# Two attentions of a second transformer block on one Trainium2 core: outputs with features on partitions, value products in pairs, and the forgetting attention alone before the output projection

## Chip, cores and metric

The kernel runs on one core of one Trainium2 chip. It is one launch that computes two transformer-like blocks on 512 tokens of width 1024, in float32. The metric is the device time of the launch in microseconds, the median of three runs. The sizes that recur below: 128 partitions, 64 features per head, query blocks of 128 tokens.

## What is computed

The first block (window attention, a long convolution by Fourier transform, differential attention, gates and a feed-forward part) is untouched by the change. The second block is this:

```python
h = rmsnorm(x, attn_norm_g)
fq, fk, fv, f_logit, sq, sk, sv = split(h @ w_in)      # 8 heads of 64 in each kind
# forgetting attention ("fox"), causal, softmax over keys
logits = fq . fk / 8 + F[t] - F[s];   p = softmax(logits, s <= t);   o_fox = p @ fv
# stick-breaking attention ("stick"), strictly causal, a reversed running sum over keys
z = sq . sk / 8
A = exp(log_sigmoid(z) + sum over s < j < t of log_sigmoid(-z[t, j]));   o_sb = A @ sv
o = concat(rmsnorm(o_fox) * fox_out_g, rmsnorm(o_sb) * sb_out_g)       # each over 512 features
x = x + o @ w_out
x = x + (silu(gate) * val) @ w_down      # gate, val = conv3(rmsnorm(x) @ w_up)
return rmsnorm(x, final_norm_g)
```

## The kernel before

**Dense products.** Every product with a weight matrix is a "group" of slots. A slot is two 128-row tiles of the weight, 512 columns wide. SyncE streams it from memory into `wraw`, ScalarE rounds it to a high part `whi` (L1489), VectorE subtracts to get the low part `wlo` (L863), and TensorE multiplies three times (high with high, low with high, high with low), so that a slot costs 24 products with 512 columns. The activations are kept the same way: `hThi`/`hTlo` for the normed input, `ohi`/`olo` for the attentions' output, `achi`/`aclo` in the feed-forward part.

**Work beside it.** The class `Flow` interleaves that with step-wise work. `Flow.pump(n)` advances the first generator of the list `beside` by n steps in each slot; `rate` of a group is that n, and the steps are spread over a slot's blocks. `Flow.drain()` runs what is left with no products between. All five engine programs (`tensor_program` for PE, `vector_program` for DVE, `scalar_program` for ACT, `gpsimd_program` for POOL, `sync_program` for SP) run the same groups and generators in the same order, so a step has one place on every engine. Nothing else sets the order.

**The two attentions.** `stick()` has 37 steps and `fox()` 38; each handles 32 units, a unit being one head of one query block n (its keys are 128 (n + 1) wide). A unit of `stick()` runs through: scores (PE, into bank 4 or 5, with a masking product), copy `zb` (ACT L1791), `parts` (DVE L1299, L1300), two logarithm steps (ACT L1796, L1798), running sum `sums` (DVE L1307), addition (POOL L2158), exponential (ACT L1803), `turn` (PE: up to four 128x128 transposes of `Lb` into bank 6), `evac` (DVE L1315, to `PT`) and `values` (PE, `PT` as the stationary side, 64 columns of `sv` moving). A unit of `fox()`: scores (PE `Kf,Qf`), row minimum `lowest` (DVE L1340), exponential with its sum (ACT L1832), `turn`, evacuation (DVE L1348 for even units, ACT L1840 for odd ones) and `values` with `fv`. Its score banks in the drain are 0, 1 and 2, its turns go to banks 4 and 5 by turns, and its values to 6 and 7. It stops at step 3 until `fox_go`, which is set after the group fv.

Both attentions run a query block at a time through their norms. Values lie with tokens on partitions, so for each block ACT squares and sums, POOL makes the root and scales (L2143), PE turns four tiles back (`out_norm_turn`), and ACT (L1781) and DVE (L1269) write `ohi` and `olo`. The fox softmax is divided once per block, in that path (L1356, L1361).

**The order around it.** Groups of the second block: sq, sk, fl (the forgetting logits, with a small running sum), sv at rate 1, fq at rate 2, fk at rate 4, fv at rate 4, each of 4 slots save fl; then the drain of `fox()`; then the output projection, `xs0`/`xs1` for the stick half of its rows and `xf0`/`xf1` for the fox half, into one set of banks; then the token norm (POOL's squares `sqs`, L2103 and L2105, PE's `token_squares` and `spread_roots`), 11 groups vp and two groups vd, in which `x_back` adds the residual by products of `xT` with the identity.

```python
def pump(self, n=1):
    for _ in range(n):
        if self.beside:
            try:
                next(self.beside[0])
s_units = [(n, h) for n in (3, 0, 2, 1) for h in range(8)]
pairs = [(n, h) for two in ((3, 0), (2, 1)) for h in range(8) for n in two]
group("fq", hT, h_ready(2), ..., 2)
group("fk", hT, h_ready(2), ..., 4)
```

Of the kernel before, what the change touches and what calls it, by code (L numbers as in the profile page):

```python
# [136 lines left out]
def counts(run):  # L137

    done, bank, n, turn = {}, {}, 0, 0
    for name, nk, cols, mode in run:  # L140
        done[name] = n
        n += 4 if mode == "tok" else cols // 128
        two = name[:2] in ("wo", "up", "dn", "xs", "xf", "vp", "vd")
# [8 lines left out]
def build(nc, d, out):  # L152
# [26 lines left out]
    def col(name, i=0, n=1, p=128):  # L179
# [89 lines left out]
    PT2 = [sb(f"PT2_{i}", AR + 124 + 2 * i, [128, 512]) for i in range(2)]  # L269
# [16 lines left out]
    in_vec, in_z, in_w3, in_dec, in_tab, in_inv = (  # L286
        sem(n) for n in ("in_vec", "in_z", "in_w3", "in_dec", "in_tab", "in_inv"))
    in_x = [sem(f"in_x{i}") for i in range(4)]
    in_res, in_mask, in_late, out_done = (
        sem(n) for n in ("in_res", "in_mask", "in_late", "out_done"))  # L290
# [39 lines left out]
    x_qk, x_mx, x_ex, x_tr, x_ea, x_ev, x_pv, x_nv = (  # L330
        sem(n) for n in ("x_qk", "x_mx", "x_ex", "x_tr", "x_ea", "x_ev", "x_pv", "x_nv"))
    o_c, o_sq, o_sc, o_tr, o_hi, o_lo = (sem(n) for n in ("o_c", "o_sq", "o_sc", "o_tr", "o_hi", "o_lo"))
    w_y, w_0, w_1 = (sem(n) for n in ("w_y", "w_0", "w_1"))
# [35 lines left out]
    s_units = [(n, h) for n in (3, 0, 2, 1) for h in range(8)]  # L369
    pairs = [(n, h) for two in ((3, 0), (2, 1)) for h in range(8) for n in two]  # L370
# [5 lines left out]
    def tensor_program(t):  # L376
# [15 lines left out]
        def group(name, act, ready, freed, rate=1, more=False, beside=None, last=True):  # L392
            first, n_s, n, mode = PLACE[name]
            for s, b, end in slots(flow, name, rate, nothing):
# [6 lines left out]
                if s == 1 and beside:  # L401
                    beside(b, bank)
                for kk in range(2):
# [3 lines left out]
                    if mode == "tok":  # L407
# [3 lines left out]
                        mm(o, ahi[:, rows], whi[h][:, c0:c1], s == 0 and kk == 0 and not more, False)  # L411
                        mm(o, ahi[:, rows], wlo[h][:, c0:c1], False, False)
                        op = mm(o, alo[:, rows], whi[h][:, c0:c1], False, last and end and kk == 1)
                    else:
                        c0 = kk * n + b * 128
                        o = ps[bank][:]
                        mm(o, whi[h][:, c0:c0 + 128], ahi, s == 0 and kk == 0 and not more, False)
# [24 lines left out]
        def x_turned():  # L442

            w.wait_ge(in_res, 16)
# [67 lines left out]
        def hyena():  # L512
            for o in range(2):
# [22 lines left out]
                w.wait_ge(in_inv, 32)  # L536
# [133 lines left out]
        def out_norm_turn(q, bank):  # L670
            w.wait_ge(o_sc, 3 * q + 3)
            take(bank)
            for k in range(4):
                op = across(bank, k, W5[5][:, k * 128:(k + 1) * 128])
            op.then_inc(o_tr, 1)
            free[bank] = [(o_lo, q + 1)]

        def stick():
            w.wait_ge(qk_c, 8)

            def scores(u):

                n, wd = s_units[u][0], 128 * (s_units[u][0] + 1)
                for i in range(2):
                    take(4 + i)
# [16 lines left out]
            def values(u):  # L702
                n, h = s_units[u]
                w.wait_ge(s_ev, u + 1)
                w.wait_ge(sv_c, n + 1)
                if h == 0:
# [4 lines left out]
                op.then_inc(s_pv, 1)  # L711
                if h == 7:
                    free[7] = [(o_c, u // 8 + 1)]

            for u in range(37):
# [4 lines left out]
                if u in (15, 23, 31):  # L720
                    out_norm_turn((u - 15) // 8, 6)
                if u >= 5:
                    values(u - 5)
# [4 lines left out]
        def fox():  # L728
            def scores(u):
                n, h = pairs[u]  # L730
                b, wd = (4, 5, 7)[u] if u < 3 else u % 3, 128 * (n + 1)
                w.wait_ge(h_p, 8)
                w.wait_ge(h_v, 8)
                w.wait_ge(in_late, 32)
# [1717 lines left out]
```

## Time and profile before

| what | value |
|---|---|
| median of 3 runs | 1698.64 us (1698.61 to 1698.65) |
| the profiled execution, its own time | 1700.36 us |
| its span | 1698.5 us, 19241 instructions |
| granted TensorE clock, mean of the span | 0.991 |
| busy: PE, DVE, ACT, POOL | 1633.2, 883.5, 645.4, 366.1 us |
| start of fq / of the fox drain / of xs0 / of vp0 | 1101.25 / 1232.26 / 1276.67 / about 1321 us |

The span is the time from the first to the last instruction in the profile; the execution's own time has what lies around it, 1.9 us here. "Busy" counts overlapping instructions of one engine once. A row of the timeline joins instructions of one form that follow each other; its second number is from the first one's start to the last one's end, and since ends of products overlap with the next start, prices are best taken from start to start.

### The profile page before, as it was taken

How to read it: one execution, taken by the hardware profiler on the slowest of the kernel's cores; microseconds unless marked ns; L12 is line 12 of the kernel's file. 1: busy time of each engine (PE TensorE's matmuls, PEld its weight loads, DVE VectorE, ACT ScalarE, POOL GpSimd, SP SyncE). 2: the span in 40 equal slices, each digit the busy share in tenths (PEclk: the TensorE clock that was granted, in tenths of full speed). 3: DMA queues.
4: the chain of work that ended last, by engine and by line, in shares of the span. 5: the costliest groups of instructions: out<-in, count | busy, mean ns of one | idle time of the engine just before them, and what ended most of it. 6: DMA issues, size and time to landing. Idle time of an engine off the chain costs nothing.

```text
span 1698.5 us, 19241 instructions
## 1 busy us (share of the span) xinstructions
PE 1633.2 (96%) x7582; PEld 1292.9 (76%) x7582; DVE 883.5 (52%) x1401; ACT 645.4 (38%) x1106; POOL 366.1 (22%) x318
## 2 busy tenths in 40 slices
PE   5999998988999999999999999998999999999998
PEld 3566787766767788888888887775788888888886
DVE  5446555366357555444343324587564767777222
ACT  4332223355445433333322212466563444444222
POOL 3444214364012116111110205033202400000000
PEclk9999998999999999999999999999999999999999
DMA  6121112211221323233333322321102232332322
GB/s 231 51 74 37 50 55 75 87 57 56 75 63 50 112 88 98 92 95 99 99 100 94 94 98 70 112 63 38 44 7 76 86 98 90 97 99 87 124 88 73
DMA packets 39221, 139.51 MB, mean 82 GB/s; under 512 B 4331, under 2 KB 4971, under 8 KB 38940
## 3 DMA queue, kind: packets, MB, share of 16 engines
q1 hardware_dynamic: 39132, 138.29, 25.3%
q8 instruction: 60, 0.98, 0.2%
q14 instruction: 29, 0.24, 0.0%
HBM read 136.14 MB, written 2.10 MB: 81 GB/s over the span
## 4 chain that ended last, share of the span: by engine, by line
PE 83%; DVE 6%; POOL 5%; ACT 3%; issue 3%; DMA 1%; SPq 0%; POOLq 0%; DVEq 0%; ACTq 0%
PE ps L387 80%; PE ps L390 3%; POOL sqs L2105 2%; POOL sqt L2103 1%; DVE raw L1056 1%; ACT whi L1489 1%; DVE W L1307 0%; DVE wlo L863 0%; DVE T L1089 0%; DMA wraw<-in_ws 0%; DMA x<-in_x 0%; POOL Lb L2158 0%; DVE tp L1051 0%; DVE sd L962 0%; DVE raw L1043 0%
## 5 line engine op out<-in xcount | busy, mean ns | idle before, releaser
L863 DVE TENSOR_TENSOR wlo<-wraw,whi 128x1024 fp32r<-128x1024 f32 (+2 forms) x220 | 271.8, 1240 | 442.7 <-ACT whi L1489 442.0
L387 PE MATMUL ps<-hThi,whi 128*128 128x512 f32 x1128 | 455.0, 403 | 1.6 <-DVE skT L1394 0.9
L387 PE MATMUL ps<-hThi,wlo 128*128 128x512 f32 x1128 | 441.5, 391 | 0.0
L387 PE MATMUL ps<-hTlo,whi 128*128 128x512 f32 x1128 | 440.9, 391 | 0.0
L1489 ACT ACTIVATE whi<-wraw 128x1024 fp32r<-128x1024 f32 (+2 forms) x244 | 251.9, 1037 | 481.9 <-PE ps L387 467.9
L387 PEld LDWEIGHTS ps<-hThi,whi 128*128 128x128 f32 x1128 | 212.9, 189 | 57.5 <-issue 16.2
L387 PEld LDWEIGHTS ps<-hTlo,whi 128*128 128x128 f32 x1128 | 213.0, 189 | 45.5 <-issue 3.6
L387 PEld LDWEIGHTS ps<-hThi,wlo 128*128 128x128 f32 x1128 | 212.6, 188 | 45.3
L387 PE MATMUL ps<-whi,hThi 128*128 128x512 f32 (+1 forms) x224 | 90.1, 402 | 6.8 <-DVE wlo L863 6.8
L387 PE MATMUL ps<-whi,hTlo 128*128 128x512 f32 (+1 forms) x224 | 85.9, 383 | 0.0
L387 PE MATMUL ps<-wlo,hThi 128*128 128x512 f32 (+1 forms) x224 | 85.8, 383 | 0.0
L2242 POOL TENSOR_TENSOR small<-small,vec 128x1 f32<-128x1 f32 x4 | 2.2, 540 | 355.0 <-DVE small L1469 355.0
L1956 POOL TENSOR_TENSOR wlo<-wraw,whi 128x1024 fp32r<-128x1024 f32 x24 | 59.1, 2463 | 85.5 <-ACT whi L1489 85.5
L2122 POOL TENSOR_TENSOR ft<-ft,R 128x512 f32<-128x512 f32 x22 | 27.9, 1290 | 199.1 <-ACT ft L1729 199.1
L387 PE MATMUL ps<-whi,achi 128*128 128x512 f32 x176 | 69.2, 393 | 0.0
L387 PE MATMUL ps<-wlo,achi 128*128 128x512 f32 x176 | 68.5, 389 | 0.0
L387 PE MATMUL ps<-whi,aclo 128*128 128x512 f32 x176 | 68.5, 389 | 0.0
L387 PE MATMUL ps<-achi,whi 128*128 128x512 f32 x176 | 68.5, 389 | 0.0
L387 PE MATMUL ps<-aclo,whi 128*128 128x512 f32 x176 | 68.5, 389 | 0.0
L387 PE MATMUL ps<-achi,wlo 128*128 128x512 f32 x176 | 68.5, 389 | 0.0
L387 PEld LDWEIGHTS ps<-whi,hThi 128*128 128x128 f32 x224 | 43.7, 195 | 21.3 <-issue 7.7
L1740 ACT ACTIVATE ft<-vt,vec 128x512 f32<-128x512 f32 x44 | 34.9, 813 | 51.0 <-DVE vt L1245 51.0
(323 smaller groups left out, 2605.7 us busy)
## 6 DMA issues: line engine op xcount, KB each, us to landing
wraw<-in_ws SPq DMA_DIRECT2D x236, 512.0 KB, 3.5
x<-in_x SPq DMA_DIRECT2D x4, 512.0 KB, 7.5
x<-in_x SPq DMA_DIRECT2D x1, 2048.0 KB, 8.4
out<-ys SPq DMA_DIRECT2D x8, 256.0 KB, 2.2
dec<-in_dec SPq DMA_DIRECT2D x1, 1024.0 KB, 15.9
wraw<-in_ws SPq DMA_DIRECT2D x4, 256.0 KB, 2.6
vec<-in_vec SPq DMA_DIRECT2D x1, 788.0 KB, 4.7
w<-in_w SPq DMA_DIRECT2D x1, 512.0 KB, 14.3
```

The costliest lines, as they stand in the source:

```text
L387: return t.matmul(o, l, r, start=first, stop=last)
L390: return t.transpose(ps[b][:, c * 128:(c + 1) * 128], src, ident)
L863: v.tensor_tensor(wlo[h][:, 0:width(i)], wraw[h][:, 0:width(i)], whi[h][:, 0:width(i)].bitcast(F32), ALU.subtract).then_inc(lo_done[h], 1)
L1056: v.tensor_tensor(r_, q0, q1, ALU.add).then_inc(r_a, 1)
L1489: a.activation(whi[h][:, 0:width(i)], wraw[h][:, 0:width(i)], ACT.Copy).then_inc(hi_done[h], 1)
L1740: a.activation(ft[i][:], vt[q % 4][:], ACT.Identity, bias=col("cb2", c), scale=col("cw2", 88 + c)).then_inc(v_a, 1)
L1956: g.tensor_tensor(wlo[h][:, 0:width(i)], wraw[h][:, 0:width(i)], whi[h][:, 0:width(i)].bitcast(F32), ALU.subtract).then_inc(lo_done[h], 1)
L2103: g.tensor_tensor(sqt[:], xT[:, f, :], xT[:, f, :], ALU.mult).then_inc(p_acc, 1)
L2105: g.tensor_tensor(sqs[:], sqs[:], sqt[:], ALU.add).then_inc(p_acc, 1)
L2122: g.tensor_tensor(t[:], t[:], R1[:], ALU.mult).then_inc(u_sr, 1)
L2242: g.tensor_tensor(small[:, 8 + b:9 + b], small[:, 4 + b:5 + b], col("mhalf"), ALU.pow).then_inc(n_rs, 1)
```

## The change

**Order.** `fox()` no longer shares fq and fk with the end of `stick()`: fq goes from rate 2 to rate 4, `fox()` is listed only after fk, and stops at step 5 until fv is done. By counting steps, `stick()` does its steps 4 to 35 in the 8 slots of fq and fk, one more in fv, and fox the rest of fv's steps, its units 5 to 31 being left to the drain.

**Units.** Both attentions go by pairs of heads: `s_units` now walks for each pair of head pairs through the query blocks 3, 2, 1, 0. Eight units give 128 features of all 512 tokens. Stick scores still use banks 4 and 5; fox scores now use them too, and all turns of both go to bank 6.

**Values.** Two heads share partitions: 64 columns of `sv` or `fv` are the stationary side, `PT` is the moving side with 128 columns, and the second head of the pair writes partitions 64 to 127 of bank 7. The output is thus born with features on partitions, and the turn behind the norm is gone (`out_norm_turn`, `out_norm_low`, `out_norm_high`, `out_norm_scale`, L1269, L1361, L1775, L1781 and L2143 with it).

**Norms.** Per eight units ACT writes `ohi` with the gain and squares the bank (`head_high`), DVE writes `olo` (`head_low`), POOL adds the squares (`head_sums`). PE sums over features (`head_squares`), DVE takes means, POOL the roots, PE spreads them (`head_roots`), DVE copies them into `Ro`. The norm is applied behind the projection: `xs0`/`xs1` are closed in banks of their own, multiplied by `Ro[0]` and added to `xT` (`projected`), and the evacuation of `xf0`/`xf1` multiplies by `Ro[1]` first. Fox softmax rows are divided unit by unit on DVE, ahead of the turn (a reciprocal and a scaling).

**x_back.** In vd0 and vd1 the products of `xT` with the identity in float32 become transposes, at the first slot rather than the second.

Some semaphores are merged. No transfer is added, dropped or moved past another.

```diff
-    s_units = [(n, h) for n in (3, 0, 2, 1) for h in range(8)]
-    pairs = [(n, h) for two in ((3, 0), (2, 1)) for h in range(8) for n in two]
+    s_units = [(n, h) for j in range(4) for n in (3, 2, 1, 0) for h in (2 * j, 2 * j + 1)]
...
             def values(u):
                 n, h = s_units[u]
-                w.wait_ge(s_ev, u + 1)
+                w.wait_ge(s_ev, u + 2)
...
-                    op = mm(ps[7][:, h * 64:(h + 1) * 64], PT2[u % 2][:, k * 128:(k + 1) * 128], sv[:, k, h * 64:(h + 1) * 64],
-                            k == 0, k == n)
+                    for i in range(2):
+                        op = mm(ps[7][64 * i:64 * i + 64, n * 128:(n + 1) * 128], sv[:, k, (h + i) * 64:(h + i + 1) * 64],
+                                PT2[(u + i) % 3][:, k * 128:(k + 1) * 128], k == 0, k == n)
...
+                if n == 0:
+                    free[7] = [(o_lo, u // 8 + 1)]
...
             def scores(u):
-                n, h = pairs[u]
-                b, wd = (4, 5, 7)[u] if u < 3 else u % 3, 128 * (n + 1)
+                n, h = s_units[u]
+                b, wd = 4 + u % 2, 128 * (n + 1)
...
             def turn(u):
-                wd, b = 128 * (pairs[u][0] + 1), 4 + u % 2
-                w.wait_ge(x_ex, u + 1)
-                take(b)
+                wd = 128 * (s_units[u][0] + 1)
+                w.wait_ge(x_sh, 2 * u + 2)
+                take(6)
...
-        flow.beside.append(fox())
-        group("fq", ..., 2)
-        group("fk", ..., 4)
+        group("fq", ..., 4)
+        group("fk", ..., 4)
+        flow.beside.append(fox())
         group("fv", hT, h_ready(2), lambda b: (fv_c, b + 1), 4)
...
                 for k in range(4):
-                    mm(ps[bank][:, k * 128:(k + 1) * 128], xT[:, 4 * half + k, b * 128:(b + 1) * 128], ident, False, False)
+                    t.matmul(ps[bank][:, k * 128:(k + 1) * 128], xT[:, 4 * half + k, b * 128:(b + 1) * 128], ident,
+                             start=k == 0, stop=False, is_transpose=True)
...
+        def head_high(q, gname):
+            w.wait_ge(s_pv if q < 4 else x_pv, 8 * (q % 4) + 8)
+            a.activation(ohi[:, q, :], ps[7][:], ACT.Copy, scale=col(gname, q % 4)).then_inc(o_hi, 1)
+            if q % 4 > 1:
+                w.wait_ge(z_p, 5 * (q // 4) + q % 4 - 1)
+            dst = osq if q % 4 else oss[q // 4]
+            a.activation(dst[:], ps[7][:], ACT.Square).then_inc(o_sq, 1)
...
+        def projected(half):
+            def evac(b, p, done):
+                f, t = 4 * half + b, px[b % 2]
+                w.wait_ge(z_row, 2)
+                v.tensor_tensor(t[:], p[:], Ro[0][:], ALU.mult).then_inc(e_s, 1)
+                v.tensor_tensor(xT[:, f, :], xT[:, f, :], t[:], ALU.add).then_inc(e_s, 1)
```

Order of instructions on PE in the group fq beside `stick()`, before: `whi`, `wlo` are weight parts, `Lb` a unit's weights to be turned, `PT2` the turned ones.

```order
L387 MATMUL ps3<-hThi_49,whi2_56 128x512
L387 MATMUL ps3<-hTlo_50,whi2_56 128x512
L387 MATMUL ps3<-hThi_49,wlo2_59 128x512
L390 MATMUL ps6<-vec_60,Lb1_199 128x128 x4
L387 MATMUL ps7<-sv_180,PT2_0_192 128x64 x4
L387 MATMUL ps0<-hThi_49,whi0_54 128x512
L387 MATMUL ps0<-hTlo_50,whi0_54 128x512
```

Twelve products stand between two steps of `stick()` there. The same engine, in fq after the change:

```order
L391 MATMUL ps0<-hThi_49,wlo2_59 128x512
L394 MATMUL ps6<-vec_60,Lb0_206 128x128 x4
L391 MATMUL ps4<-skT_179,sqT_178 128x256
L391 MATMUL ps5<-skT_179,sqT_178 128x256
L391 MATMUL ps4<-mkR_205,identR_204 128x128
L391 MATMUL ps5<-mkR_205,identR_204 128x128
L391 MATMUL ps1<-hThi_49,whi2_56 128x512
L391 MATMUL ps1<-hTlo_50,whi2_56 128x512
L391 MATMUL ps1<-hThi_49,wlo2_59 128x512
L391 MATMUL ps1<-hThi_49,whi2_56 128x512
L391 MATMUL ps1<-hTlo_50,whi2_56 128x512
L391 MATMUL ps1<-hThi_49,wlo2_59 128x512
L394 MATMUL ps6<-vec_60,Lb1_207 128x128 x4
```

Now a turn comes every six products, each into bank 6.

PE in the fox drain, before (`Tf` is a unit's softmax part, `PTf` the turned one):

```order
L387 MATMUL ps2<-Kf_184,Qf_183 128x128
L390 MATMUL ps4<-vec_60,Tf2_208 128x128 x4
L387 MATMUL ps6<-fv_185,PTf0_212 128x64 x4
L387 MATMUL ps0<-Kf_184,Qf_183 128x512
L390 MATMUL ps5<-vec_60,Tf3_209 128x128
L387 MATMUL ps7<-fv_185,PTf1_213 128x64
L387 MATMUL ps1<-Kf_184,Qf_183 128x128
```

and after:

```order
L394 MATMUL ps6<-vec_60,Tf3_217 128x128
L391 MATMUL ps4<-Kf_184,Qf_183 128x384
L394 MATMUL ps6<-vec_60,Tf4_218 128x128 x4
L391 MATMUL ps5<-Kf_184,Qf_183 128x384
L391 MATMUL ps7<-PTf2_222,fv_185 64x128
L391 MATMUL ps7<-PTf3_223,fv_185 64x128
L394 MATMUL ps6<-vec_60,Tf5_219 128x128 x4
L391 MATMUL ps4<-Kf_184,Qf_183 128x256
L394 MATMUL ps6<-vec_60,Tf0_214 128x128 x3
```

Turns went from two banks to one, scores from three banks to two, and wide units no longer alternate with narrow ones. DVE in the same drain, after:

```order
L1391 RECIPROCAL st2_203<-st2_203 128x1
L1393 TENSOR_SCALAR Tf4_218<-Tf4_218,st2_203 128x384
L1306 SCALAR_TENSOR_TENSOR olo_182<-ps7,vec_60,ohi_181 128x512
L1385 ISA Tf0_214,st2_203<-ps4,mk_202 128x256
L1385 ISA st2_203 128x1
L1391 RECIPROCAL st2_203<-st2_203 128x1
L1393 TENSOR_SCALAR Tf5_219<-Tf5_219,st2_203 128x384
L1400 COPY PTf2_222<-ps6 128x384
```

Before, DVE did the row minimum of each unit and every second evacuation here, and four `olo` parts of 128 per query block; the reciprocal and the scaling per unit are new.

## Rows read from the trace of the kernel before

**Rows 1.** The page, busy time of the engines over the span

```profile
PE 1633.2 (96%) x7582; PEld 1292.9 (76%) x7582; DVE 883.5 (52%) x1401; ACT 645.4 (38%) x1106; POOL 366.1 (22%) x318
```

**Rows 2.** Stretches: length; busy PE, PEld, DVE, ACT, POOL; clock; DMA share, GB/s

```profile
1101.25:1141.05 39.80, 38.98 (x223) 31.35 (x222) 32.72 (x43) 25.41 (x46) 15.54 (x13) 1.00 0.23 66
1141.05:1211.75 70.70, 60.19 (x310) 44.53 (x309) 52.81 (x101) 45.15 (x111) 27.54 (x33) 0.93 0.12 38
...
1211.75:1232.26 20.51, 20.28 (x100) 16.36 (x101) 8.39 (x16) 8.72 (x18) 2.91 (x5) 1.00 0.25 77
1232.26:1276.67 44.41, 43.66 (x311) 36.54 (x310) 27.38 (x92) 26.13 (x91) 2.86 (x6) 1.00 0.00 1
```

**Rows 3.** PE timeline in the fox drain (start, us, engine, line, what, count)

```profile
1239.50 0.27 PE L390 MATMUL ps<-vec,Tf 128*128 128x128 f32 x1
...
1240.49 1.00 PE L387 MATMUL ps<-fv,PTf 128*128 128x64 f32 x8
1241.33 1.08 PE L387 MATMUL ps<-Kf,Qf 66*128 66x512 f32 x2
1242.25 0.27 PE L390 MATMUL ps<-vec,Tf 128*128 128x128 f32 x1
```

**Rows 4.** PE timeline in the first block's window attention, whose values go in pairs

```profile
406.10 0.88 PE L387 MATMUL ps<-PT,va 128*64 128x128 f32 x12
406.90 0.50 PE L387 MATMUL ps<-whi,hThi 128*128 128x512 f32 x1
```

**Rows 5.** DVE by line, 1080 to 1300 us: busy, mean ns | idle before

```profile
L1307 DVE TENSOR_TENSOR_SCAN W<-W,Lb 128x512 f32<-128x512 f32 (+3 forms) x32 | 29.4, 918 | 1.8 <-ACT Lb L1798 1.7
L1299 DVE SCALAR_TENSOR_TENSOR Lb<-zb 128x512 f32<-128x512 f32 (+3 forms) x32 | 24.6, 769 | 12.8 <-ACT zb L1791 12.8
L863 DVE TENSOR_TENSOR wlo<-wraw,whi 128x1024 fp32r<-128x1024 f32 x20 | 24.4, 1221 | 19.2 <-ACT whi L1489 19.2
L1315 DVE COPY PT<-ps 128x512 f32<-128x512 f32 (+3 forms) x32 | 15.1, 473 | 5.0 <-PE ps L390 4.9
L1340 DVE CUSTOM_DVE_ANT_0 Tf<-ps,mk 128x512 f32<-128x512 f32 (+3 forms) x32 | 15.1, 487 | 18.0 <-PE ps L387 18.0
L1300 DVE TENSOR_SCALAR W<-zb 128x512 f32<-128x512 f32 (+3 forms) x32 | 12.5, 392 | 0.0
```

**Rows 6.** DVE by line and form, window attention: per-unit reciprocal and scaling

```profile
L1099 DVE TENSOR_SCALAR T<-T,st 128x256 f32<-128x256 f32 x16 | 5.9, 370 | 0.6
...
L1097 DVE RECIPROCAL st<-st 128x1 f32<-128x1 f32 x32 | 5.2, 164 | 1.1
```

**Rows 7.** ACT by line, 1080 to 1300 us: fox exponential, and a copy out of PSUM

```profile
L1832 ACT ACTIVATE Tf<-Tf,st 128x512 f32<-128x512 f32 (+3 forms) x32 | 17.8, 557 | 18.2 <-DVE st L1340 18.1
...
L1762 ACT ACTIVATE fv<-ps,small 128x512 f32<-128x512 f32 x4 | 2.6, 678 | 0.7 <-PE ps L387 0.7
```

**Rows 8.** PE timeline in fk: scores with mask, and a turn that waits

```profile
1180.78 0.70 PE L387 MATMUL ps<-skT,sqT 64*128 64x256 f32 x4
1181.41 0.44 PE L387 MATMUL ps<-mkR,identR 128*128 128x128 f32 x2
1181.69 0.83 PE L387 MATMUL ps<-sv,PT 128*128 128x64 f32 x6
...
1188.68 0.52 PE L390 MATMUL ps<-vec,Lb 128*128 128x128 f32 x3 [2.24 <-DVE PT L1315]
```

**Rows 9.** PE timeline in vd0: `x_back` between products

```profile
1632.03 0.39 PE L387 MATMUL ps<-whi,aclo 128*128 128x512 f32 x1
1632.26 1.05 PE L387 MATMUL ps<-vec,xT 128*128 128x128 f32 x8
1633.06 0.48 PE L387 MATMUL ps<-whi,achi 128*128 128x512 f32 x1
```

**Rows 10.** PE timeline in vp0: the token norm's sums

```profile
1332.94 1.05 PE L387 MATMUL ps<-ones,sqs 128*128 128x1 f32 x8 [0.63 <-POOL sqs L2105]
1333.86 0.48 PE L387 MATMUL ps<-hThi,whi 128*128 128x512 f32 x1
```

More of the change, by code:

```diff
@@ L410, in group @@
                         o = ps[bank][:, 0:n]
-                        mm(o, ahi[:, rows], whi[h][:, c0:c1], s == 0 and kk == 0 and not more, False)
+                        mm(o, ahi[:, rows], whi[h][:, c0:c1], s == 0 and kk == 0 and not (more or beside), False)
                         mm(o, ahi[:, rows], wlo[h][:, c0:c1], False, False)
@@ L764, in fox @@
+                if n == 0:
+                    free[7] = [(o_lo, 4 + u // 8 + 1)]
+            for u in range(36):
+                while u == 5 and not fox_go:
                     yield
+                if 3 <= u < 35:
+                    turn(u - 3)
                 if u < 32:
                     scores(u)
[L767 to L771 removed]
+                if u == 5:
+                    head_squares(0, 6)
+                if u == 9:
+                    head_roots(0, 6)
+                if u >= 5 and u % 2:
@@ L836, in tensor_program @@
         for half in range(2):
-            group("xs%d" % half, lambda k: (ohi[:, k, :], olo[:, k, :]), lambda k, b: w.wait_ge(o_lo, 4), lambda b: None,
-                  last=False)
-        residual("xf%d", 3, lambda k: (ohi[:, 4 + k, :], olo[:, 4 + k, :]), lambda k, b: w.wait_ge(o_lo, 8), more=True)
+            group("xs%d" % half, lambda k: (ohi[:, k, :], olo[:, k, :]), lambda k, b: w.wait_ge(o_lo, k + 1),
+                  lambda b: (e_s, 8 * half + 2 * b + 1), 1)
+        flow.drain()
+        flow.beside.append(fox_norm())
+        for half in range(2):
+            group("xf%d" % half, lambda k: (ohi[:, 4 + k, :], olo[:, 4 + k, :]), lambda k, b: w.wait_ge(o_lo, 4 + k + 1),
+                  lambda b: (e_s, 16 + 4 * half + b + 1), 4)
         flow.later(2, lambda: token_squares(3, 0))
@@ L1452, in vector_program @@
         for half in range(2):
-            group("xs%d" % half, none)
-        residual("xf%d", 3, "g4")
+            group("xs%d" % half, projected(half), 1)
+        flow.drain()
+        flow.beside.append(fox_norm())
+        residual("xf%d", 3, "g4", 4)
         flow.later(2, lambda: means(3, 0))
@@ L1927, in scalar_program @@
         for half in range(2):
-            group("xs%d" % half, none)
-        residual("xf%d", 3, "g4")
+            group("xs%d" % half, none, 1)
+        flow.drain()
+        flow.beside.append(iter(range(5)))
+        residual("xf%d", 3, "g4", 4)
         ffn("vp", 3)
@@ L2233, in gpsimd_program @@
         for half in range(2):
-            group("xs%d" % half, none)
-        residual("xf%d", 3)
+            group("xs%d" % half, none, 1)
+        flow.drain()
+        flow.beside.append(fox_norm())
+        residual("xf%d", 3, 4)
         flow.later(2, lambda: spread(3))
```

350 lines of the change are left out of this document (180 added, 170 removed).

## Prediction

> **What bounds the kernel now.** I read the busy shares first: PE is busy 96% of the span, DVE 52% [rows 1]. That says PE almost everywhere, but it is a mean over unlike stages, so I read the stretches that the change touches [rows 2]. fq (39.8 us) and the fox drain (44.4 us) are full of PE, and so is the end of fv. The 70.7 us from fk into fv are not: PE 60.2, DVE 52.8, ACT 45.2, and a granted clock of 0.93. There PE waits at turns, and the row that ends such a wait is DVE's copy out of bank 6 (2.24 us) [rows 8]. So here the loop turn, copy, next turn, with DVE's other work ahead of the copy, sets the pace. In the drain the timeline shows PE dense: two units, a wide and a narrow one, take 1242.25 - 1239.50 = 2.75 us with no wait noted [rows 3].
>
> The forecast is made against the profiled execution, 1700.36 us (span 1698.5 and 1.9 around it), and the difference is carried over to the median of the runs, 1698.64, which lies 1.7 lower. 0.2% is 3.4 us, about what a measurement of this kernel can tell from no change.
>
> **Paired value products.** Before, eight of them take 1241.33 - 1240.49 = 0.84 us, 0.105 each [rows 3]; an attention has 32 units of 2.5 on average, 80 of them, 8.4 us. The first block has the new form already: twelve, six pairs, take 0.80, 0.133 a pair [rows 4]; 40 pairs are 5.3. So PE saves 3.1 us per attention. That is real where PE is the limit, and nothing where it waits.
>
> **A. fq, fk and fv with stick beside (131.0 us before, the first three stretches of [rows 2]).** `stick()` now has to do 32 units in 8 slots, that is eight units (128 features of all tokens) in two slots. Cost of such a group of eight:
> - PE: 48 products at 0.23 [rows 9] are 11.0. Twenty transposes at 0.11 are 2.2 (four scores and a transpose apart, one transpose holds 0.11 of [rows 3]); four score pairs at the 0.91 that 256 wide ones take with their masks (1181.69 - 1180.78) [rows 8], rather more for the mean width, 4.1; ten value pairs 1.3; re-entries of products after smaller ones, and the rest, about 2.5. Together about 21.
> - DVE: per unit 0.918 + 0.769 + 0.473 + 0.392 = 2.55 [rows 5], for eight 20.4; two `wlo` at 1.22, 2.4; one `head_low`, at the 0.68 that ACT's 512-wide copy takes [rows 7], 0.7. Together 23.5. Before, DVE did less per slot in fq (rate 2) and the same in fk.
>
> DVE's work is thus more than PE's, at less than full coupling. I walked one group with the instruction order of the change and these prices, each wait taken as late as its last releaser: the turn on PE waits for DVE's copy from bank 6, DVE's sum for ACT's logarithms, ACT for POOL's addition, which waits for DVE's sum. Without the head it closes in 23.2, so DVE is the pace. At the end of each eight, bank 7 has to be read: values (PE), then ACT's copy 0.68 [rows 7] in its turn among the exponentials, then DVE's `head_low`, which stands in DVE's queue ahead of the next `parts` and copies; behind it PE's turns and ACT's and POOL's next units. That adds 2.3: 25.5. Four groups are 102, with 2 for the evacuations of fq and fk (Qf, Kf): 104. fv then has 96 products, 22.0, five fox scores (3.7 by 0.92 for a 512-wide one [rows 3], less for narrower ones), two turns 0.9, stick's last step 0.6: 27.3. Sum 131.3, against 131.0: +0.3. The half-speed clock of before (0.93 over 70.7 us, the lower of the two levels, 1.2 GHz, for about 10 us, after PE had waited at turns) is likely again with PE at 21 of 25.5, and I take 1.2 for its being spread wider. **A = +1.5.**
> Bounds: PE alone, 4 x 21 + 27.3 = 111.3, -19.7. DVE's busy time (4 x 23.5 and 5.5 for Qf and Kf) stretched as in fk, 70.7 / 52.8 = 1.34 [rows 2]: 133 + 27.3, +29. I stay near DVE's own time because in fq DVE ran at 32.7 of 39.8 with PE the limit, so it can be this full.
>
> The Trainium skill, page "TensorEngine Tiling (Array Packing)", section "PSUM Bottleneck", says "Tiling speeds up TensorE but not PSUM evacuation". That speaks against the change; [rows 8] agree, a turn waiting for a copy. If PE's saving counted in full instead, A would be 3.1 us lower than with none of it.
>
> **B. The fox drain (44.4 before).** Per eight units DVE now has 8 row minima at 0.487 and four copies at about 0.473 [rows 5], and new, per unit, a reciprocal 0.164 and a scaling at 0.37 [rows 6]: 3.9 + 1.9 + 4.3 = 10.1, 9.1 where starts overlap; `head_low` 0.7. PE has about 9. All turns go to bank 6, so each waits for the copy of the one before, and every second copy is ACT's (0.3 to 0.7), which stands there behind an exponential of 0.557 [rows 7]. The walk gives 11.9 per eight, and 1.3 at each head (ACT's copy and square of bank 7, both about 0.68, before the next values). Three groups at 13.2 are 39.6; the first one is partly done in fv, 5.5 left; the roots at step 9 wait for POOL, 1.85; the last values, copy and `olo` 2.6. Sum 49.6: **B = +5.2.**
> Bounds: with PE as the limit the drain loses pairs (3.1), five norm turns (2.2) and what fv took over (about 2.5): 36.6, -7.8. With DVE at 10.8 and its stretch of 1.34: 4 x 14.5 less the part in fv, about 53, +9. I take the walk, since [rows 3] show today's PE without slack only because two turn banks and wide and narrow units by turns kept DVE ahead.
>
> **C. Output projection and its norms.** Removed here: two norm turns (0.44 each). Added: `head_squares` as `token_squares`, 0.92 (1333.86 - 1332.94), and a spread of about 0.9: +0.9. The extra evacuation steps of xs on DVE lie beside 12 us of products and cost nothing; if that cover were gone they would be eight times 1.4. At the last block of xf1 DVE multiplies before it adds, so POOL's squares start one DVE step (0.7) later, and PE already waits 0.63 for them [rows 10]; with POOL's queue also holding the head's work, 1.2. **C = +2.1**, between 0.9 and 4.
>
> **D. x_back.** Eight products now take 1633.06 - 1632.26 = 0.80 [rows 9]; four transposes are 0.44. Eight blocks, all on PE, which is the limit there: 8 x 0.36, **D = -2.9**. Bounds: -2 to -3.2.
>
> Sum 1.5 + 5.2 + 2.1 - 2.9 = **+5.9**: 1704.5 us.
>
> **Rivals.**
> 1. *Faster: the loops stay loose.* If the heads of eight cost nothing (ACT's copy comes early enough, the next unit's work fills DVE), a group in A takes DVE's 23.2 and in the drain 11.9. A is 4 x 23.2 + 2 + 27.3 = 122.1, -8.9; B 5.5 + 3 x 11.9 + 1.85 + 2.6 = 45.7, +1.3; with C and D -8.4: 1690. It decides from 24.0 us per group in A downward (B, C and D as forecast). For it: fq before ran with PE full and DVE at 82% [rows 2]; there are five `Lb` buffers. Against: the wait of 2.24 us at half that density [rows 8]. The Trainium skill, page "TensorEngine Tiling (Array Packing)", section "Performance Considerations", advises swapping the sides and tiling by columns where the moving side is 64 wide, which would give this sign. Chance 0.32.
> 2. *No change*: A gains the 3 to 4 us that B loses, within 3.4 of 1698.6. Chance 0.20.
> 3. *Pairs do not overlap*: if the two halves of a pair went one after the other, 160 products of 0.105 to 0.16 add 6 to 14 us on PE and the time is about 1710. Against it, 0.133 a pair [rows 4]. The first product behind the pairs takes 0.50 there, and 0.48 behind `x_back` or the token sums [rows 4, 9, 10], so nothing is lost on leaving them. The Trainium skill, same page, section "Key Properties", says that a change of tiling mode drains TensorE. Chance 0.03.
> 4. *Much slower*: A's groups stretch as fk does now (1.34 on DVE), with more time at 1.2 GHz; over 1715. Chance 0.09.
> The forecast itself, 1702 to 1715: 0.36.
>
> **Numbers.** Slower by over 0.2%: forecast 0.36, rivals 3 and 4 0.12, less a little that lies under 1702: 0.47. Same 0.21, faster 0.32. The range takes in rival 1 with 3 us below it, and all of the forecast: 1687 to 1717.
>
> **What the profile after would show.** Right: fq starts at the same time; fq and fk together near 104 us with DVE at 90% and waits of turns ended by DVE's copy; waits of PE at every eighth unit ended by `olo`; a drain of 49 us in which PE is at 80% and waits for copies or for the scaling; x_back 0.45 a block. Wrong: a group of eight under 24 us (rival 1); PE dense in the drain; transposes in `x_back` slower than 0.2 each; or a stretch at 0.5 of the clock in the drain, where PE's idle time would then cost twice.

## The result and the profile after

The changed kernel takes 1726.2 us (median of 4 runs, 1720.39 to 1730.43) against 1698.62: a ratio of 1.0163, 95% interval 1.0131 to 1.0196. It is slower by 27.6 us where 5.9 were forecast, and outside the range (1687 to 1717). Its runs lie further apart than those of the kernel before (1696.29 to 1698.65), and they order by the mean granted TensorE clock of each: 1720.39 at 0.981, 1722.29 at 0.979, 1730.12 and 1730.43 at 0.972. The run profiled below is the fastest of them, 1720.39 us with a span of 1718.6, so the profile holds 20.1 of the 27.6 us.

Busy time on the page, beside [rows 1], and the clock in 40 slices:

```profile
PE 1636.0 (95%) x7538; PEld 1278.3 (74%) x7538; DVE 912.3 (53%) x1461; ACT 642.7 (37%) x1070; POOL 364.8 (21%) x304
...
PEclk9999998999999999999999999998988999999999
```

PE has 44 instructions fewer and is busy for 2.8 us more. Stretches of the changed kernel, columns as in [rows 2]: first and second half of fq with fk, fv, the fox drain, the output projection, the start of vp:

```profile
1100.29:1154.19 53.90, 45.82 (x261) 32.67 (x260) 40.91 (x69) 34.77 (x74) 18.79 (x19) 0.94 0.16 50
1154.19:1209.83 55.64, 46.35 (x254) 32.74 (x253) 43.88 (x69) 31.99 (x69) 21.98 (x23) 0.88 0.12 39
1209.83:1237.16 27.33, 27.01 (x120) 20.86 (x119) 12.82 (x27) 11.51 (x20) 2.46 (x2) 1.00 0.25 77
1237.16:1293.13 55.97, 45.62 (x297) 28.76 (x295) 34.12 (x130) 26.98 (x76) 4.61 (x4) 0.86 0.00 1
1293.13:1340.90 47.77, 47.77 (x205) 39.08 (x203) 33.40 (x39) 12.22 (x14) 13.88 (x10) 0.95 0.24 73
1340.90:1363.54 22.64, 19.75 (x84) 15.78 (x82) 17.13 (x17) 5.94 (x8) 14.81 (x10) 0.92 0.32 103
```

The clock has two levels, so a mean of 0.88 over 55.64 us is 2 x 0.12 x 55.64 = 13 us at 1.2 GHz. Summed like that for each kernel (with the clock's records to a tenth of a microsecond), the stretches compare so:

| stretch | before, us (at 1.2 GHz) | changed, us (at 1.2 GHz) | difference | forecast |
|---|---|---|---|---|
| fq and fk | 95.0 (10.2) | 109.5 (20.5) | +14.5 | |
| fv | 36.0 (0) | 27.3 (0) | -8.7 | |
| fq to fv | 131.0 | 136.9 | +5.9 | A, +1.5 |
| fox drain | 44.4 (0) | 56.0 (15.6) | +11.6 | B, +5.2 |
| xs and xf | 44.6 (0) | 47.8 (4.9) | +3.2 | C in part, +0.9 |
| vp0 to the end | 377.2 (4.0, at the end) | 377.7 (7.6) | +0.5 | C, rest, +1.2, and D, -2.9 |
| before fq | 1101.2 | 1100.3 | -1.0 | 0 |

### The profile page after: what moved, and what is told of

Same layout as the page of the kernel before. It is cut to its first block, busy times and chain, and to the rows that moved or that the text cites. A ratio compares the mean times of both kernels' runs of the same rounds, so it can differ in the third digit from the quotient of the medians.

```text
span 1718.6 us, 19204 instructions
## 1 busy us (share of the span) xinstructions
PE 1636.0 (95%) x7538; PEld 1278.3 (74%) x7538; DVE 912.3 (53%) x1461; ACT 642.7 (37%) x1070; POOL 364.8 (21%) x304
## 4 chain that ended last, share of the span: by engine, by line
PE 81%; DVE 8%; POOL 4%; issue 3%; ACT 3%; DMA 1%; SPq 0%; POOLq 0%; DVEq 0%; ACTq 0%
PE ps L391 78%; PE ps L394 3%; POOL sqs L2150 1%; POOL sqt L2148 1%; ACT whi L1549 1%; DVE W L1351 1%; DVE wlo L892 1%; DVE raw L1085 1%; POOL Lb L2210 0%; DVE Lb L1343 0%; DVE T L1118 0%; DVE Tf L1385 0%; DMA wraw<-in_ws 0%; DVE tp L1080 0%; DMA x<-in_x 0%
## 5 line engine op out<-in xcount | busy, mean ns | idle before, releaser
L391 PEld LDWEIGHTS ps<-hThi,wlo 128*128 128x128 f32 x1128 | 213.7, 189 | 45.5
## 6 DMA issues: line engine op xcount, KB each, us to landing
w<-in_w SPq DMA_DIRECT2D x1, 512.0 KB, 13.4
```

The costliest lines, as they stand in the source:

```text
L391: return t.matmul(o, l, r, start=first, stop=last)
```

## Experiments

All times are medians, beside the kernel before on the same chip (1697.07 to 1698.08 us). "Changed" is the changed kernel, 1726.2. Where two kernels ran on different chips, their difference is taken from the distance of each to the kernel before on its own chip; the changed kernel's distance is 27.6. Times of stages are those of one profiled execution.

**x_back alone**, on the kernel before:

```diff
-                if s == 1 and beside:
+                if s == 0 and beside:
...
-                    mm(ps[bank][:, k * 128:(k + 1) * 128], xT[:, 4 * half + k, b * 128:(b + 1) * 128], ident, False, False)
+                    t.matmul(ps[bank][:, k * 128:(k + 1) * 128], xT[:, 4 * half + k, b * 128:(b + 1) * 128], ident,
+                             start=k == 0, stop=False, is_transpose=True)
```

> The kernel before with the transposes in x_back alone. If an x_back block is worth what the prediction says (0.80 us to 0.44), the time falls by 2.9 us, to about 1695.7, and nothing else moves. If transposes into a bank that the products then add to are dearer, or if the waits of the first slot come in, it falls by less than 1.5 us. Either way this term can't carry the 28 us.

1694.85 against 1697.72 us, ratio 0.9985 (0.9976 to 0.9995): -2.9, between -4.1 and -0.8. In the timeline of PE in vd0 of the changed kernel a block is even shorter than priced, 0.35 us (1649.07 - 1648.72) for 0.80 in [rows 9]:

```profile
1648.72 0.60 PE L877 MATMUL ps<-vec,xT 128*128 128x128 f32 x4
1649.07 0.48 PE L391 MATMUL ps<-whi,achi 128*128 128x512 f32 x1
```

The term holds. It is the only part of the change that was shown to pay by itself; the order alone (below) does not, and the layout and the units were not tried alone.

**Two banks for fox's turns**, on the changed kernel:

```diff
+    def turned(u):
+        return 3 if u > 5 and u % 2 else 6
...
-                take(6)
+                b = turned(u)
+                take(b)
...
-                v.tensor_copy(PTf[u % 4][:, 0:wd], ps[6][:, 0:wd]).then_inc(x_ev, 1)
+                v.tensor_copy(PTf[u % 4][:, 0:wd], ps[turned(u)][:, 0:wd]).then_inc(x_ev, 1)
```

> The changed kernel with the turns of the fox drain by turns in banks 6 and 3 (from unit 6 on). Theory A, the single turn bank makes the drain slow: the drain (56.0 us in the changed kernel's profile) falls to about 48 and the waits of turns for the copies (ACT L1891, 7.0 us) go. Theory B, the drain is bound by DVE and ACT (row minimum, exponential, reciprocal, scaling, copy, one behind the other): the waits go over to the scaling (DVE L1393) and the drain falls by under 3 us. Theory C, half of the loss is the granted clock (44 us at the lower level from fq to vp0, against 10 before): a denser drain has less of it, and xs0 too gets about 2.5 us back.

1711.91 us, ratio to before 1.0081 (1.0066 to 1.0097): 14.2 over the kernel before, so 13.4 of the 27.6 us are gone with one bank. The drain went from 56.0 to 46.9 us, and xs with xf from 47.8 to 45.5; neither has time at 1.2 GHz any more. Set beside the 50.0 us of the filler below, which is at full clock with one turn bank, about 6 of the drain's 9.1 us are the clock and 3 the bank itself. Theories A and C both got their numbers. Waits of PE in the changed kernel's drain (us in total, times, longest):

```profile
PE ps L394 <- ACT PTf L1891: 7.0, 7, 1.7
PE ps L394 <- DVE st L1391: 1.3, 3, 0.4
```

and its timeline over one group of eight units:

```profile
1259.71 1.02 PE L391 MATMUL ps<-Kf,Qf 66*128 66x512 f32 x2
...
1268.14 0.52 PE L394 MATMUL ps<-vec,Tf 128*128 128x128 f32 x3 [1.64 <-ACT PTf L1891]
...
1272.91 1.02 PE L391 MATMUL ps<-Kf,Qf 66*128 66x512 f32 x2
```

The group at full clock takes 1272.91 - 1259.71 = 13.20 us, the 13.2 of the prediction's walk, and the turn waits for ACT's copy, as walked. What the walk did not have is time at half speed: 3.4 us in the group before this one, and everything from 1280.9 us on, most of the last group and the tail.

**Two banks for fox's values**, on the changed kernel with its one turn bank:

```diff
+    def valued(q):
+        return 2 if q in (5, 7) else 7
...
-                        op = mm(ps[7][64 * i:64 * i + 64, n * 128:(n + 1) * 128], fv...
+                        op = mm(ps[b][64 * i:64 * i + 64, n * 128:(n + 1) * 128], fv...
```

> The changed kernel with the values of fox in bank 7 and bank 2 by turns of eight units, so that the next eight need not wait for ACT's copy and square and DVE's low part. If the prediction's price of the head (1.3 us a group of eight in the drain, three groups) is right, the drain falls by 3 to 4 us. If DVE's queue, in which the low part waits for ACT's square in any case, is what waits there, it falls by under 1 us.

1724.93 us, within the runs of the changed kernel. The drain is 57.0 us here, with 20.5 at 1.2 GHz where the changed kernel has 56.0 with 15.6, and PE still waits 5.3 us at its turns for ACT's copy. At the price of the clock that the filler gives (about 0.4 us for each at 1.2 GHz), an estimate of what the bank saves is 1 us: nothing that can be told from none, the second case.

**The order alone**, on the kernel before:

```diff
-        flow.beside.append(fox())
-        group("fq", ..., 2)
+        group("fq", ..., 4)
         group("fk", ..., 4)
+        flow.beside.append(fox())
```

> The kernel before with the order of groups alone: fq at rate 4, fox listed after fk. Old layout, old units, old banks. If the order is what costs (denser steps of stick in fq and fk, with PE waiting for DVE's copies and the clock falling), fq and fk together go from 95.0 to about 107 us, fv gets shorter by 8 or so, and the whole is 5 to 12 us slower than before. If layout and units cost, it stays within 3 us of before.

1700.52 us, ratio 1.002 (1.0008 to 1.0032): +2.8. fq with fk 108.5 us, fv 24.5, in sum 133.0 against 131.0. With the old layout the denser order thus costs 2 to 3 us, a tenth of the loss, and has 6.8 us at 1.2 GHz there, not 20. The whole came out as in the second case, within 3 us, although fq and fk grew as in the first: fv gave back more than expected. By elimination layout, units and banks have the rest. No run changes the order of the units or the layout of the values alone, so how it splits between those two stays open.

**Filler in the drain**, on the changed kernel:

```diff
+                for c in range({2: 12, 1: 3, 4: 3}.get((u - 3) % 8, 0) if 7 <= u < 35 else 0):
+                    across(1, c % 4, ident)
                 if 3 <= u < 35:
                     turn(u - 3)
```

> The changed kernel with extra transposes of the identity into the unused bank 1 ahead of the turns of the fox drain that wait (twelve for the third unit of each eight, three for the second and fifth), so that PE is busy in its waits. They are 4 x 18 x 0.11 us = 8 us of PE time, most of it inside waits. If the lower clock of the drain and of xs0 (20.5 us at 1.2 GHz in the changed kernel's profile) comes from those waits, it goes, the drain falls from 56.0 to about 51, xs and xf from 47.8 to 45.5, and the whole by 5 to 9 us. If the clock does not follow PE's waits, nothing is gained or the time rises by 1 to 2 us.

1715.14 us, ratio 1.0104 (1.0089 to 1.0119): 58 matmul records more in the drain, and 9.5 us less in the whole (18.1 over the kernel before, for 27.6). The drain's row:

```profile
1238.09:1288.11 50.02, 45.83 (x355) 30.82 (x353) 33.89 (x130) 26.90 (x76) 4.62 (x4) 1.00 0.01 2
```

No time at 1.2 GHz, 50.02 us: the prediction's 49.6 for the drain. xs with xf fell to 45.5 as well, since part of their first microseconds had been slow too. This is the cleanest reading of the clock's part: 15.6 us at half speed inside the drain cost 6.0 us there, or somewhat more, since the filler may itself delay a turn; 4.9 in xs cost 2.3.

**fq back at rate 2**, on the changed kernel:

```diff
-        group("fq", ..., 4)
+        group("fq", ..., 2)
```

> The changed kernel with fq back at rate 2, so that stick runs on into fv, as fox did before. If stick is too dense in fq and fk (PE waits for DVE's copies, 17 us, and 20 us at the lower clock), fq, fk and fv together fall from 136.9 to 129 to 132 us; what is under 131.0 would be the gain of the paired products and of the missing norm turns. If DVE's total is what counts, whatever the spread, they stay within 2 us of 137.

1719.6 us (1714.78 to 1726.19). fq to fv took 135.7 us, within 2 us of 137, the second case, though five kernels with the old rate 4 and the same stick have 139.6 to 139.8. But the drain behind it took 65.1 in the profiled run, the slowest of the four, with a mean clock of 0.974 (0.979 to 0.983 in the others):

```profile
1250.00:1294.40 44.40, 42.00 (x174) 25.88 (x175) 22.97 (x84) 17.64 (x50) 2.53 (x2) 0.50 0.00 1
```

Here PE is busy for 42.0 of 44.4 us and stays at the lower level all the time. What it did before: in the drain's first 15.3 us, at full clock, it was idle for 2.9 us; the clock fell inside a wait of 1.70 us for ACT's copy. From then on the products took about twice as long and the waits mostly closed, to 2.4 us in 44.4. Why the level stayed low with PE that busy isn't shown.

The Trainium skill, page "TensorE: Matmul & The Clock Gate", Part 1, says that the gate is set by how busy PE has been recently; its loops that fall and rise again match the changed kernel, whose clock falls six times between 1100 and 1300 us, and this row, slow with a PE that hardly idles, shows a case that such a rule alone would not lead one to expect.

**Without the per-unit division**, with two turn banks:

```diff
-                if 1 <= u <= 32:
-                    shares(u - 1)
...
-                w.wait_ge(x_sh, 2 * u + 2)
+                w.wait_ge(x_ex, u + 1)
```

> Two turn banks as in e2_turn_banks, and fox's reciprocal and scaling per unit left out: the forgetting attention's rows are not divided by their sums. If DVE's new work per unit is what keeps e2's drain at 46.9 us, it falls to 41 or less (32 x 0.53 us of DVE are gone, PE becomes the limit at about 37 plus the heads' waits of 1.24 each). If the heads and PE set it, it falls by under 2 us.

The rows of fox stay undivided here. 1707.72 us; the drain falls from 46.9 to 43.4, between the two cases (41 or less, and 45 or more). DVE's busy time there falls from 33.2 to 21.0 us, so 12 us less on DVE give 3.5 us. DVE's new work has a price, but the loop is not bound by DVE's total.

**Both pairs of banks:** e2_turn_banks and e3_value_banks together.

> e2_turn_banks and e3_value_banks together. In e2 the wait at the head shows as PE's values waiting 1.24 us for DVE's low part, three times. If a second value bank hides it now that the turns no longer do, the drain falls by 3 to 4 us from e2's 46.9, to 43.3, under the 44.4 of before. If another wait takes its place (the turns behind it, by DVE's queue), it falls by under 1.5.

1711.18 us, drain 46.9: as e2 alone. In e2 PE's values wait three times for DVE's low part:

```profile
1268.19 1.09 PE L394 MATMUL ps<-PTf,fv 128*64 128x128 f32 x16 [1.24 <-DVE olo L1310]
```

With a second bank that wait goes elsewhere: PE's waits in the drain are 6.3 us in sum, for 6.7 in e2, but now for ACT's copies (3.1, for 0.7) and DVE's row minima (2.0, for 1.1). DVE still stands still for 4.1 us at `olo` until ACT has squared, and PE then waits for what is queued behind it.

**Filler in stick**, on e9_both_banks:

```diff
+                if 4 <= u < 36 and (u - 4) % 8 in (1, 2):
+                    take(4)
+                    for c in range(12):
+                        across(4, c % 4, ident)
                 if 4 <= u < 36:
                     turn(u - 4)
```

> e9_both_banks with twelve extra transposes of the identity (1.3 us, into bank 4, which the scores then overwrite) ahead of the second and third turn of each eight units of stick, where PE waits 2.2 to 2.4 us for DVE's copy. Clock theory: the 27 us at 1.2 GHz in fq and fk shrink to 10 or less, and fq and fk fall from about 112 us to 106 or less. If these waits are not what lowers the clock, or DVE alone sets the pace, fq and fk stay at 111 to 113.

1707.6 us, 3.6 less. Rows of fq with fk, for e9_both_banks:

```profile
1101.44:1213.71 112.27, 94.57 (x513) 67.39 (x512) 83.52 (x137) 66.84 (x143) 40.55 (x41) 0.88 0.14 43
```

and with the filler:

```profile
1098.92:1207.46 108.54, 97.25 (x609) 72.44 (x608) 85.26 (x137) 66.54 (x143) 40.84 (x41) 0.97 0.14 45
```

96 instructions more, 3.7 us less; time at 1.2 GHz from 27.3 to 6.8. Its expectation named 106 us or less: the clock came as expected, the time did not. DVE (85.3 us for 83.5) and POOL are hardly busier, so a loop of waits still sets the pace. The filler itself is about 10 us of PE work (96 at 0.11, an estimate), and how much of the clock's gain it takes back wasn't tested.

**The low part a step later**, on e9_both_banks:

```diff
-                if u >= 12 and u % 8 == 4:
+                if u >= 13 and u % 8 == 5 or u == 36:
                     head_low((u - 12) // 8, "gsb")
...
-                if u >= 11 and u % 8 == 3:
+                if u >= 12 and u % 8 == 4 or u == 35:
                     head_low(4 + (u - 11) // 8, "gfox")
```

> e9_both_banks with DVE's head_low one step later in both attentions, so that DVE does another unit's work while ACT copies and squares bank 7. The prediction priced this wait at 2.3 us a group of eight in stick (the trace shows DVE idle 1.25 us there, and PE waiting 2.2 and 2.4 us for copies behind it). If that is the price, fq and fk fall by 4 to 8 us, with the clock perhaps more; if DVE's order of work alone makes PE wait, they fall by under 2 us.

1705.83 us, 5.4 less: fq with fk 108.3 (from 112.3) and the drain 44.4 (from 46.9, and equal to the kernel before). The drain is at full clock in both, so its 2.5 us are the wait itself. In fq with fk the two can't be told apart:

```profile
1097.73:1206.03 108.30, 90.25 (x514) 63.72 (x512) 85.77 (x137) 66.68 (x143) 41.30 (x41) 0.94 0.14 44
```

PE does the same work in 90.3 us instead of 94.6, since its time at 1.2 GHz went from 27.3 to 13.7, and it is idle for as long as before (18.1 and 17.7 us). What it changes is to be seen on DVE in the changed kernel:

```profile
1131.37 0.67 DVE L1360 COPY PT<-ps 128x512 f32<-128x512 f32 x1
1131.95 0.85 DVE L1343 SCALAR_TENSOR_TENSOR Lb<-zb 128x256 f32<-128x256 f32 x1
1132.73 0.28 DVE L1344 TENSOR_SCALAR W<-zb 128x256 f32<-128x256 f32 x1
1134.26 0.75 DVE L1306 SCALAR_TENSOR_TENSOR olo<-ps,vec,ohi 128x512 fp32r<-128x512 f32 x1 [1.25 <-ACT oss L1842]
1134.92 0.95 DVE L1351 TENSOR_TENSOR_SCAN W<-W,Lb 128x384 f32<-128x384 f32 x1
1135.79 0.67 DVE L1360 COPY PT<-ps 128x512 f32<-128x512 f32 x1
```

and on PE, waiting on either side of it:

```profile
1132.18 0.63 PE L394 MATMUL ps<-vec,Lb 128*128 128x128 f32 x4 [2.19 <-DVE PT L1360]
...
1136.60 0.52 PE L394 MATMUL ps<-vec,Lb 128*128 128x128 f32 x3 [2.42 <-DVE PT L1360]
```

DVE waits for ACT's copy and square of bank 7, then has the low part and a running sum to do, and only then the copy for which PE's next turn waits. 1.25 us of idle time on an engine that is busy for 77% of the stage, with the two instructions behind it, hold up PE for 2.42. (The wait of 2.19 came before, and so had nothing to do with this low part.) In e11 DVE no longer waits at `olo`.

**The copy first**, on e9_both_banks:

```diff
-                if 2 <= u < 34:
-                    sums(u - 2)
                 if 4 <= u < 36:
                     evac(u - 4)
+                if 2 <= u < 34:
+                    sums(u - 2)
```

> e9_both_banks with DVE doing the copy out of bank 6 ahead of the running sum in each step of stick. The copy then stands 0.6 to 1.1 us earlier in DVE's queue, and the turn that waits for it too. If the single bank 6 between PE and DVE is the loop that sets the pace, fq and fk fall by 4 to 10 us. If the loop over DVE's sum, POOL's addition and ACT's exponential is, the sum now comes later, and they rise by 2 or more.

1719.79 us, 8.6 more than e9: fq with fk 117.6. The waits of PE for DVE's copy rose from 17.7 to 24.2 us:

```profile
PE ps L400 <- DVE PT L1368: 24.2, 11, 3.3
```

DVE's own wait at the copy for PE did not rise (8.0 us, for 10.0). What rose are ACT's waits for POOL's addition (50.1 us, for 28.2), and DVE's for ACT's `whi` (13.9, for 5.8). The second case: the sums come later, and with them POOL and ACT; that the long way through the four engines is as tight as the short one between PE and DVE is the reading that fits.

**Banks and rate 2:** e9_both_banks with fq at rate 2.

> e9_both_banks with fq at rate 2. In e6_rate fq, fk and fv took 135.7 us in sum, but the drain behind them ran at 1.2 GHz for 44 of 65 us. If the single turn bank let the clock stay low there, the drain is now 42 to 44 us, without a stretch at 1.2 GHz, and the whole comes out 2 to 5 us under e9, near 1707. If the lower clock comes from how fv ends, the drain is over 55 us again.

1707.4 us (1704.22 to 1710.54), 3.8 less than e9, as expected, though the intervals overlap; the drain is 46.9 (42 to 44 were expected) with a clock of 1.00, and the four runs have mean clocks of 0.987 and 0.988. So e6's 44 us at half speed did not come back with the second banks. fq to fv are 137.4 with 20.5 us at 1.2 GHz, for e9's 139.6 with 27.3; spreading by itself gives little.

**Filler in the kernel before**, on e1_xback:

```diff
+                if u - 4 in (17, 20, 22, 28):
+                    take(4)
+                    for c in range(9):
+                        across(4, c % 4, ident)
```

> e1_xback (the kernel before with the transposes in x_back) with nine extra transposes of the identity into bank 4 ahead of the four turns of stick, units 17, 20, 22 and 28, where PE waits 0.6 to 2.2 us. If the lower clock follows PE's waits, in the old order too, the 7 to 10 us at 1.2 GHz in fk go and the time is 2 to 4 us under e1_xback's (1694.9), near 1692. If the old order's clock has another cause, the four fillers cost up to 2 us and give nothing.

1693.93 us, ratio to before 0.9971 (0.9959 to 0.9983); e1 had 0.9985 (0.9976 to 0.9995). Time at 1.2 GHz in fk fell from 6.8 to 3.4. The difference to e1, 1.3 us where 2 to 4 were expected, is not resolved; the clock's worth there is small. This is the best version measured.

**Low part later, both fillers,** on e11_low_later, with this in `token_squares`:

```diff
+            take(bank)
+            for c in range(20 if n == 3 else 0):
+                across(bank, c % 4, ident)
             w.wait_ge(p_acc, 17 * n - 1)
-            take(bank)
```

> e11_low_later with the filler of e10_filler_stick, and twenty transposes of the identity ahead of the wait of token_squares in vp0. fq and fk fall from 108.3 to 103 to 105, near the 104 of the prediction, with under 7 us at 1.2 GHz; the 6.8 us at 1.2 GHz in vp go, for 2 to 3.4 us; the whole is near 1699. If heads and clock overlap in what they cost, fq and fk stay above 107.

1702.57 us, 4.5 over the kernel before for e11's 8.7: 4.2 less. The part in vp came out: no time at 1.2 GHz after vp0 but at the very end, and 2.9 us less from vp0 on. The part in stick did not: fq with fk 107.7 with 10.2 us still slow, not 103 to 105. The filler takes 3.4 us of half speed away here, where it took 20.5 from e9; most of that the later low part had already taken.

**The same at rate 2:** e15_low_fill with fq at rate 2.

> e15_low_fill with fq at rate 2. If the spread of stick over fq, fk and fv is worth something by itself once clock, banks and heads are mended, it comes out 2 to 5 us under e15, near or under the kernel before (1697). If DVE's total is what counts, it is within 2 us of e15.

1701.82 us, ratio 1.002 (1.0011 to 1.0028), against e15's 1.002 (1.0011 to 1.0029): no difference. fq to fv are 91.5 + 41.5 = 133.0 us in its profile, the drain 44.3, and it is still 3.7 us over the kernel before, 6.6 over e1_xback. With banks, heads and clock mended, where stick's steps are put is thus not what costs.

## Why the prediction was wrong

**What bounds the kernel.** Right in kind: between fq and fv a loop of waits, in which PE's turn waits for DVE's copy, sets the pace. In the changed kernel that wait sums to 17.4 us over fq and fk:

```profile
PE ps L394 <- DVE PT L1360: 17.4, 10, 3.9
```

**A, +1.5; measured +5.9 in the fastest run, and more in the others.** The walk gave 104 us for fq and fk; the changed kernel has 109.5 and five more kernels with the same stick 112.3 to 112.5. With filler it is 108.5, and 107.7 to 108.3 with the head mended. So the sum is 5 to 8 us short, and still 4 with 7 to 14 us left at 1.2 GHz; no run has the stage at full clock. The failing step is "The half-speed clock of before ... is likely again ... and I take 1.2 for its being spread wider". It was to be 20 to 27 us in place of 10. Even 10 us would have been more than 1.2: the 104 is walked at full clock, and at the 0.4 us that the filler in the drain gives for each us at half speed they cost about 4 (an estimate). A second step was wrong though it cost little: "Together 23.5", DVE's work for eight units. DVE is busy for 40.9 + 43.9 = 84.8 us over fq and fk, under the 99.5 of the sum; its records alone, taken line by line, sum to 93.7, so overlaps are most of the gap. DVE was not the pace; the way around the loop was. That the walk, with DVE too dear and the clock too cheap, came within 5.5 us is in part luck. fv's 27.3 was right to the tenth.

**B, +5.2; measured +11.6.** Here the mechanism and the size held, and the failing step is one that isn't in the sum at all: no clock was priced for the drain. A group of eight took 13.20 us as walked, the drain with filler 50.0 against 49.6 walked. The prediction had named it only among the signs of an error ("a stretch at 0.5 of the clock in the drain, where PE's idle time would then cost twice"), with no price, and gave "about 53" as the upper end. The rest of the 27.6 us over this profile, 7.5, goes with the clock of the other runs (0.972 for 0.981); there are no traces of them, so where it falls isn't shown. The five kernels with the same stick give a hint: they have 2.9 us more in fq and fk than this profile and 1.4 more from vp0 on. If the slower runs are like them, 4.3 of the 7.5 lie there and some 3 in the drain.

**C, +2.1; measured +0.9 in the projection without the clock (45.5 for 44.6), and in vp about +2.2 more wait.** The token squares:

```profile
1354.80 1.05 PE L391 MATMUL ps<-ones,sqs 128*128 128x1 f32 x8 [2.86 <-POOL sqs L2150]
```

2.86 us for the 0.63 of [rows 10], where 1.2 was put on it, and behind it 3.4 us (6.8 in most experiments) at 1.2 GHz. Mis-sized by the wait and by the clock. Where the wait comes from stands at the end.

**D, -2.9; measured -2.9 alone, by its rows 8 x 0.45 = -3.6.** Right.

**The paired products.** Price and form held (16 records, eight pairs, from 1268.19 to the next start at 1269.22 in e2_turn_banks, 0.13 a pair), and rival 3 is out. The drain's PE work fell from 43.7 us busy to 39.4 in e15; the norm turns that are gone and what fv took over are in this too. It was saved in a stage where PE now waits.

**The rivals.** Rival 4, "Much slower ... with more time at 1.2 GHz; over 1715", had 0.09 and is what came, though by the drain as much as by A's groups, whose stretch on DVE was 109.5 / 84.8 = 1.29. Rival 1 (a loose loop) fell; by the prediction's own sum it would have made the kernel faster only under 23.5 us a group, since at the 24.0 named there the four terms leave -1.3. Nothing hangs on that: mended by banks and a later low part, groups still didn't reach 24 us on average (107.7 / 4 less the two evacuations is 26.4). The sentence of the Trainium skill, page "TensorEngine Tiling (Array Packing)", section "PSUM Bottleneck", did point to the right place: a second bank for the turns was worth 13.4 us, clock included.

**The account.** From the 27.6 us over the kernel before: a second turn bank -13.4 (with the clock that came with it; filler alone, -9.5), a second value bank -0.1, the later low part -5.4, fillers in stick and vp -4.2. That leaves 4.5 over the kernel before, 7.4 over it with x_back. Between the profiles of e16_low_fill_rate and e1_xback lie 6.3 us: 2.9 in fq to fv, 0.9 in xs and xf, 2.4 from vp0 on; the drain is level. In the end the change gains nothing in the drain or in stick even when mended, since PE's saving is taken up by waits. Whether division in another place would let the drain fall to the 43.4 of e8 wasn't tried.

## What to carry to other kernels

Before taking work off the engine that is busiest, look whether it waits in that stage; if it does, count banks and the order of the queue behind the wait, not its instructions. A PE that was full and begins to wait can lose its clock, as in this drain (15.6 us at 1.2 GHz where there had been none), and then it pays for the idle time and for the slow products behind it. It need not (the drain of e2 has waits of up to 1.2 us and keeps it): put a price on that in every stage that the change thins out, and test it with filler in the waits, which is cheap. When units are grouped so that one instruction needs the whole group, put that instruction a step after its input is ready.

## What was not expected of the hardware

- Extra work on PE made the kernel faster: 96 records more in stick gave 3.7 us, 58 more in the drain 6.0, since they kept the granted clock at 2.4 GHz for longer.
- The lower level can last with PE nearly full: 44.4 us at 0.50 with 42.0 us busy (e6_rate). It had not been seen in the kernel before, whose drain was full at 1.00.
- One DVE form takes 0.74 or 1.77 us by what POOL does. On DVE in vp0 of the changed kernel:

```profile
1342.00 0.74 DVE L1226 SCALAR_TENSOR_TENSOR hTlo<-xT,vec,hThi 128x512 fp32r<-128x512 f32 x1
...
1344.11 1.77 DVE L1226 SCALAR_TENSOR_TENSOR hTlo<-xT,vec,hThi 128x512 fp32r<-128x512 f32 x1
```

and on POOL at that time:

```profile
1342.16 1.48 POOL L2148 TENSOR_TENSOR sqt<-xT 128x512 f32<-128x512 f32 x1 [2.49 <-DVE xT L1241]
1343.72 1.61 POOL L2150 TENSOR_TENSOR sqs<-sqs,sqt 128x512 f32<-128x512 f32 x1
```

The slow one starts while POOL's addition runs, and ends just behind its end (1345.88 and 1345.33). In the kernel before the same form takes 0.88 to 1.18 us there, and these too end 0.55 us behind an instruction of POOL. POOL needs 3.1 us a block or a little more in both kernels, so this is not what made the token squares late. That is POOL's one idle time of 2.49 us in the rows above, which DVE's `xT` ends: DVE had two low parts of weights to do first, beside POOL, the second at 2.30 us where such a one takes 1.22 alone, and then the extra multiplication.

```profile
1338.45 2.30 DVE L892 TENSOR_TENSOR wlo<-wraw,whi 128x1024 fp32r<-128x1024 f32 x1
```

The Trainium skill, page "SBUF — State Buffer", section "SBUF: two separate sides", calls the pair of ports that the two engines share an exclusive lock, held for a whole instruction; these rows agree.
